# Retention constants and a buffer write issued one stage earlier, and the residual input read inside the out projection

## The chip, the cores and the metric

One NeuronCore of a Trainium2 chip runs the whole program. The metric is the device time in microseconds, as a median over runs. Everything is float32.

## The reference, cut to what matters

The reference is a chain of two transformer-like blocks over 512 tokens of width 1024 (with a context of 256 tokens in the first). The change touches the second half of the first block's mixer and nothing else:

```python
# first block, mixer: two branches over the same normed input, then one projection
r_f, _ = retention_scan(rq, rk, rv, lg_f, states[2], False)       # 4 heads, dk 128, dv 256
r_b, _ = retention_scan(flip(rq), flip(rk), flip(rv), lg_b, states[3], True)
o_ret = head_groupnorm(r_f + flip(r_b)) * silu(heads(rg, 4))
y = sigmoid(m_gla) * (o_gla @ w_branch_gla) + sigmoid(m_ret) * (o_ret @ w_branch_ret)
h_lat = x + g1 * (y @ w_out)
h_lat = h_lat + g2 * hier_moe(...)        # 32 experts, top 2
```

The retention decays depend on positions and heads alone. The kernel keeps them as three constant tables in DRAM: `ret_kdec` (8 KB, one factor per context token, head and direction), `ret_qdec` (512 KB per head once it is spread over the 128 partitions) and `ret_band` (1,792 KB, the banded mask of decays that multiplies the scores). `rope_axial` and `perm_axial` are the tables of the rotary embedding.

## The kernel before, in words

The program is a sequence of stages. Each stage is a `with nc.Block()` in which every engine has its own list of instructions. The end of a block is a barrier of all engines: nothing of the next stage starts, on any engine or on the queue of SyncE (SP), before all have come to it. TensorE writes its products to the eight banks of PSUM in turn (`env.tile()`), VectorE or ScalarE evacuates them. `product_done`, `evacuated` and `bank_ready` are waits on counters of full and free banks.

The large weights come in blocks of 2 MB into a ring of two slots, `wring` (L130, `load_blocks`). Block b may be issued when the last tile that used block b-2 is done; SP waits for that in order, so everything that stands behind it in SP's list waits too. At the end of its list each stage lets `load_blocks` run two blocks ahead of its own. `until` stops it at a given block.

The stages around the change, in order:

1. The GLA branch's `stage_branch`, which ends with VectorE's L831.
2. `stage_ret_project` (from L887): TensorE makes queries (4 tiles), keys (4 tiles), the context's keys by token (2 tiles), eight rotary products of one matmul each (L864), and the values in two halves of 6 tiles each (L951), one weight block for each half: `b_v[0]` and `b_v[1]`. Each of the tiles with weights is a sum over `KD` = 8 products, which the trace shows as 16 float32 matmuls. ScalarE evacuates, VectorE does the rotation (L874 to L881). SP's list: the two rotary tables (L906, L907), then `load_blocks`.
3. `stage_ret_core` (from L955): SP's list begins with a write of 12,288 KB to `y_dram` in DRAM (L983): row 0 of `env.gates` of every partition, repeated. It gives the buffer that the experts will later scatter into finite contents; GpSimd waits for it (`env.y_set`) only in the experts' stage, whose first scatter into it starts at 1192.5 us. Behind it stand `kdec` (L985), `band` (L986), and `qdec` for the four heads (L991), whose third and fourth wait until VectorE has used the first and second. VectorE begins with `v.wait_ge(in_s, 32)`, which is `kdec` and `band` both, then scales the context keys (L1002). TensorE makes the eight state products from these (L1060, 32 matmuls), then for each head the scores (L1067) and the outputs (L1076, L1079). VectorE multiplies the scores with the band (L1013). At the end come the group norm and transposes, which leave the result in `oT`; `oT` is the memory of `env.h`.
4. The retention branch's `stage_branch`: 24 tiles with weights; it reads `oT` and ends with VectorE's L835.
5. `load_tokens` (L2589): a block of its own, in which SP loads `x` (2,048 KB) into `env.h` again (L2596) and waits for it. The other engines have nothing in it.
6. `stage_out`: TensorE's 8 tiles of `y @ w_out` (L1123, 128 matmuls), VectorE's multiplication with the gate (L1112) and the addition to `env.h` (L1114). Its first block of weights has been issued during stage 4, its second at the end of stage 4.
7. The norm before the experts, whose first instruction is ScalarE's at 1085.89 us.

Of the kernel before, what the change touches and what calls it, by code (L numbers as in the profile page):

```python
# [20 lines left out]
ALU = mybir.AluOpType  # L21
# [3 lines left out]
P = 128  # L25
D = 1024
KD = D // P
S = 512
NT = S // P
# [855 lines left out]
def stage_ret_project(env, R):  # L885

    nc, hT, dram = env.nc, env.hT, env.dram  # L887
    q_t = env.tiles(4)
    b_q = env.take_block(q_t[-1])
    k_t = env.tiles(4)  # L890
    kc_t = env.tiles(NCT)
    b_k = env.take_block(kc_t[-1])
    r_t = env.tiles(8)
    v_t, b_v = [], []
    for half in range(2):
        v_t.append(env.tiles(NCH))
        b_v.append(env.take_block(v_t[half][-1]))
    tab_in, cos_s, rope_s = env.sem("ret_tab_in"), env.sem("ret_cos"), env.sem("ret_rope")
    with ExitStack() as st:
        sn = st.enter_context(nc.sbuf_tensor("r_sn", [P, 2, S], F32))  # L900
        tab = st.enter_context(nc.sbuf_tensor("r_tab", [P, 2, S], F32))
        perm = st.enter_context(nc.sbuf_tensor("r_perm", [P, P], F32))
        with nc.Block() as block:
            @block.sync
            def _(sp):
                nc.sync.dma_start(tab[:], dram["rope_axial"]).then_inc(tab_in, 16)  # L906
                nc.sync.dma_start(perm[:], dram["perm_axial"]).then_inc(tab_in, 16)  # L907
                load_blocks(env, sp)

            @block.scalar  # L910
            def _(act):
                for j, t in enumerate(q_t + k_t):
                    product_done(env, act, t)
                    nc.scalar.activation(R.qk[:, j, :], env.ps[:, t[0], :], ACT.Copy).then_inc(env.bank_free[t[0]], 1)
                for i, t in enumerate(kc_t):
                    product_done(env, act, t)
                    nc.scalar.activation(R.kc[:, i, :], env.ps[:, t[0], :], ACT.Copy).then_inc(env.bank_free[t[0]], 1)
                for half in range(2):
                    for i, t in enumerate(v_t[half]):
                        product_done(env, act, t)  # L920
                        nc.scalar.activation(R.v[:, i, half * WBLK:(half + 1) * WBLK], env.ps[:, t[0], :],
                                             ACT.Copy).then_inc(env.bank_free[t[0]], 1)

            @block.vector
            def _(v):
                v.wait_ge(tab_in, 32)
                rope_dve(env, v, r_t, lambda j: R.qk[:, j, :], tab, sn, cos_s, rope_s)

            @block.tensor
            def _(pe):  # L930
                w = block_view(env, pe, b_q)
                for j, t in enumerate(q_t):
                    project(env, pe, t, env.ps[:, t[0], :], w, j * P, (j + 1) * P, lambda k: hT[:, k, 0:S])
                w = block_view(env, pe, b_k)
                for j, t in enumerate(k_t):
                    project(env, pe, t, env.ps[:, t[0], :], w, j * P, (j + 1) * P, lambda k: hT[:, k, 0:S])
                for i, t in enumerate(kc_t):
                    by_token(env, pe, t, WBLK, w, NT + i)
                pe.wait_ge(tab_in, 32)
                rope_mm(env, pe, r_t, perm[:], lambda j: R.qk[:, j, :], lambda j: evacuated(env, pe, (q_t + k_t)[j]))  # L940
                for half in range(2):
                    w = block_view(env, pe, b_v[half])
                    for i, t in enumerate(v_t[half]):
                        by_token(env, pe, t, WBLK, w, i)
# [11 lines left out]
def stage_ret_core(env, R, oT):  # L956
# [3 lines left out]
    st_t = [[env.tile() for d in range(2)] for hd in range(H1)]  # L960
    plan = [([env.tile() for _ in range(NT)], [env.tile() for _ in range(NT)]) for hd in range(H1)]
    fin = env.tiles(2 * H1)
    in_s, kd_s, qd_s, bn_s, mv_s, rms_s, inv_s, nrm_s, o_s = (env.sem("rc_" + n) for n in (
        "in", "kd", "qd", "bn", "mv", "rms", "inv", "nrm", "o"))
    qdec_in = [env.sem(f"rc_qdec_in{i}") for i in range(2)]
    with ExitStack() as stk:
        T = lambda n, s: stk.enter_context(nc.sbuf_tensor("rc_" + n, s, F32))
        band = T("band", [P, H1, 896])
        qdec = T("qdec", [P, 2, 2, S])
        kdec = T("kdec", [P, 2 * H1, NCT])  # L970
        kd = T("kd", [P, 2, 2, NCT, DK])
        st = T("st", [P, H1, 2, DV])
        qd = T("qd", [P, 2, S])
# [6 lines left out]
        with nc.Block() as block:  # L980
            @block.sync
            def _(sp):
                nc.sync.dma_start(env.dram["y_dram"].rearrange("(b p) d -> p b d", p=P),  # L983
                                  env.gates[:, 0, :].unsqueeze(1).broadcast_to([P, NB, D])).then_inc(env.y_set, 16)
                nc.sync.dma_start(kdec[:], dram["ret_kdec"]).then_inc(in_s, 16)  # L985
                nc.sync.dma_start(band[:], dram["ret_band"]).then_inc(in_s, 16)  # L986
                for hd in range(H1):
                    if hd >= 2:
                        sp.wait_ge(qd_s, 2 * (hd - 1))
                    row = dram["ret_qdec"][hd:hd + 1].broadcast_to([P, 2, S])  # L990
                    nc.sync.dma_start(qdec[:, hd % 2], row).then_inc(qdec_in[hd % 2], 16)  # L991
                load_blocks(env, sp)

            @block.vector
            def _(v):
                v.wait_ge(in_s, 32)
                for hd in range(H1):
                    for d in range(2):
                        if hd >= 2:
# [4 lines left out]
                for hd in range(H1):  # L1004
                    sc, ov = plan[hd]
                    if hd >= 1:
                        product_done(env, v, plan[hd - 1][1][-1])
                    v.wait_ge(qdec_in[hd % 2], 16 * (hd // 2 + 1))
                    for d in range(2):
                        nc.vector.tensor_tensor(qd[:, d, :], R.qk[:, hd, :], qdec[:, hd % 2, d, :], ALU.mult).then_inc(qd_s, 1)  # L1010
                    for J, t in enumerate(sc):
                        product_done(env, v, t)
                        nc.vector.tensor_tensor(pm[:, J, :], env.ps[:, t[0], :], band[:, hd, 384 - J * P:384 - J * P + S],  # L1013
                                                ALU.mult).then_inc(env.bank_free[t[0]], 1)
                    for I, t in enumerate(ov):
                        product_done(env, v, t)
                        nc.vector.bn_stats(bn[:, hd * NT + I, :], env.ps[:, t[0], 0:DV]).then_inc(bn_s, 1)
# [66 lines left out]

def stage_out(env, name, src, gate):

    nc = env.nc
    tl = [env.tiles(NT) for _ in range(2)]  # L1090
    bl = [env.take_block(t[-1]) for t in tl]
    g_s = env.sem(name + "_sum")
    with ExitStack() as st:
        tmp = st.enter_context(nc.sbuf_tensor(name + "_tmp", [P, 2 * NT, WBLK], F32))
        with nc.Block() as block:
            @block.sync
            def _(sp):
                load_blocks(env, sp)

            @block.vector  # L1100
            def _(v):
                for half in range(2):
                    cs = slice(half * WBLK, (half + 1) * WBLK)
                    for i, t in enumerate(tl[half]):
                        product_done(env, v, t)
                        got = env.ps[:, t[0], :]
                        if gate is None:
                            nc.vector.tensor_tensor(env.h[:, i, cs], env.h[:, i, cs], got, ALU.add).then_inc(
                                env.bank_free[t[0]], 1)
                        else:  # L1110
                            x = tmp[:, half * NT + i, :]
                            nc.vector.tensor_tensor(x, env.gates[:, gate, cs], got, ALU.mult).then_inc(env.bank_free[t[0]], 1)  # L1112
                            evacuated(env, v, t)
                            nc.vector.tensor_tensor(env.h[:, i, cs], env.h[:, i, cs], x, ALU.add).then_inc(g_s, 1)  # L1114

            @block.tensor
            def _(pe):
# [1468 lines left out]
            env.blocks.append(a[i])  # L2586


def load_tokens(env, name, src):  # L2589

    nc = env.nc
    done = env.sem(name)
    with nc.Block() as block:
        @block.sync
        def _(sp):
            nc.sync.dma_start(env.h[:], src.rearrange("(t p) d -> p t d", p=P)).then_inc(done, 16)  # L2596
            sp.wait_ge(done, 16)


def first_mixer(env):  # L2600
    nc = env.nc
    gain = lambda n: (lambda j: env.gain[:, n, j:j + 1])
# [24 lines left out]
    with ExitStack() as own:  # L2627
        A = lambda n, s: own.enter_context(nc.sbuf_tensor(n, s, F32))
        R = Bufs()
        R.qk, R.kc, R.v = A("ret_qk", [P, 2 * H1, S]), A("ret_kc", [P, NCT, H1 * DK]), A("ret_v", [P, NCH, D])  # L2630
        stage_ret_project(env, R)
        stage_ret_core(env, R, oT)
    stage_branch(env, "ret", oT, yT, False)
    load_tokens(env, "x_again", env.dram["x"])
    env.hold = True
    stage_out(env, "mix_out", yT, 0)
    branch.close()
    mod.close()

# [248 lines left out]
```

## Time and profile before

| | us |
|---|---|
| median of 3 runs | 3281.82 |
| lowest and highest | 3277.95 and 3285.40 |
| the profiled execution's own time | 3285.16 |
| its span | 3283.3 |
| TensorE busy | 2788.1 (85% of the span) |
| VectorE busy | 1478.0 (45%) |
| ScalarE busy | 490.4 (15%) |
| GpSimd busy | 734.7 (22%) |
| mean granted TensorE clock | 0.929 |

The page of the profile cuts the span into 40 equal slices of 82 us and gives each engine's busy share in tenths. Further views are asked of the same execution: the timeline (instructions of each engine in order of time, merged where one follows another without a pause), windows (busy time of each engine in given stretches, with the clock that TensorE was granted and the DMA engines' share), and the DMA issues with the time from issue to landing. All times are microseconds from the start of the span. 1.00 of the granted clock is 2.4 GHz, 0.50 is 1.2 GHz.

### The profile page before, as it was taken

Reading aid. Unit: us, or ns where it says so; the run is one execution under the profiler, and the core shown is the slowest. Engines: PE = TensorE matmul, PEld = TensorE weight load, DVE = VectorE, ACT = ScalarE, POOL = GpSimd, SP = SyncE. Lnnn points to the kernel's source line nnn. Section 1 sums busy time; section 2 is a strip of 40 time slices with the busy share of each in tenths; the row PEclk is TensorE's granted clock in tenths of the full one; section 3 lists DMA queues with packets and bytes.
Section 4 is the critical chain, followed back from the end, with each engine's and each line's share of the span. In section 5 each row is a group of like instructions: output and inputs, shape, how many; then the busy total and the mean of one; then the engine's idle time right before and its main releaser. Section 6 shows DMA issues by size and latency. Waiting matters only on the chain. (4 is left out here: it accounts for less than half of the span.)

```text
span 3283.3 us, 30222 instructions
## 1 busy us (share of the span) xinstructions
PE 2788.1 (85%) x10080; PEld 1561.4 (48%) x10080; DVE 1478.0 (45%) x3007; ACT 490.4 (15%) x1015; POOL 734.7 (22%) x652
## 2 busy tenths in 40 slices
PE   7997899976998689977979989998990578888877
PEld 3446434435443433323435568887880443333333
DVE  1126200102201322212137429888668987777762
ACT  2124100000100111113026321111110210000002
POOL 0000000000000012220000002655457036666650
PEclk9897998997999689988989999998995999999998
DMA  5100251123022479971210026999999249999992
GB/s 201 48 30 24 103 204 59 51 98 155 26 77 77 171 320 409 391 300 72 77 65 7 1 84 243 416 402 346 419 416 372 81 193 413 413 414 413 413 363 86
DMA packets 133341, 693.93 MB, mean 211 GB/s; under 512 B 19571, under 2 KB 20979, under 8 KB 105587
## 3 DMA queue, kind: packets, MB, share of 16 engines
q1 hardware_dynamic: 50644, 408.32, 31.4%
q0 software_dynamic: 81792, 281.07, 21.7%
q10 hardware_dynamic: 800, 3.15, 0.3%
q8 instruction: 65, 1.06, 0.1%
q14 instruction: 40, 0.33, 0.0%
HBM read 701.90 MB, written 48.23 MB: 228 GB/s over the span
## 5 line engine op out<-in xcount | busy, mean ns | idle before, releaser
L428 PE MATMUL ps<-hT,wring 128*128 128x256 f32 (+1 forms) x2576 | 763.3, 458 | 30.3 <-ACT pk_g L2249 14.4
L428 PEld LDWEIGHTS ps<-hT,wring 128*128 128x128 f32 x2576 | 491.1, 191 | 297.3 <-issue 253.5
L2468 PE MATMUL ps<-pm_v_rows,pm_weighted 128*128 128x512 f32 x1024 | 464.7, 603 | 62.0 <-DVE pm_weighted L2518 44.3
L2143 POOL DMA_INDIRECT pk_ring<-in_peer_u,pk_rows x256 | 311.3, 1216 | 760.6 <-DVEq L2357 537.0
L2285 DVE CUSTOM_DVE_ANT_0 pk_ring<-pk_ring,mem_x 128x1024 f32<-128x1024 f32 x256 | 309.7, 1224 | 104.5 <-DMA pk_ring<-in_peer_u,pk_rows 99.6
L2468 PEld LDWEIGHTS ps<-pm_v_rows,pm_weighted 128*128 128x128 f32 x1024 | 185.7, 189 | 340.4 <-issue 227.6
L2436 POOL DMA_INDIRECT hT<-in_peer_v,pm_idxs x192 | 251.7, 1311 | 211.5 <-PE ps L2456 107.8
L1416 POOL COPY ex_idx<-row_token 128x1 uint32 (+1 forms) x24 | 4.5, 186 | 1283.4 <-PEq L1548 1149.9
L2524 DVE SCALAR_TENSOR_TENSOR h_tok<-hT,gates,h_tok 128x1024 f32<-128x1024 f32 x192 | 244.6, 1282 | 100.3 <-DMA hT<-in_peer_v,pm_idxs 65.0
L951 PE MATMUL ps<-wring,hT 128*128 128x512 f32 (+1 forms) x544 | 213.9, 555 | 1.2 <-PEq L376 1.2
L1603 DVE TENSOR_SCALAR hT<-ps,gain,ada 128x128 f32<-128x128 f32 x192 | 63.4, 405 | 216.2 <-PE ps L1504 216.2
L428 PE MATMUL ps<-hT,pk_u 128*128 128x256 f32 x704 | 153.8, 379 | 0.0
L951 PEld LDWEIGHTS ps<-wring,hT 128*128 128x128 f32 x544 | 98.4, 190 | 116.2 <-issue 116.2
L428 PEld LDWEIGHTS ps<-hT,pk_u 128*128 128x128 f32 x704 | 133.7, 190 | 18.3
L1514 PE MATMUL ps<-ex_gu,hT 128*64 128x512 f32 x512 | 115.8, 606 | 5.5 <-DVE hT L1603 4.3
L428 PE MATMUL ps<-h_tok,wring 128*128 128x512 f32 x256 | 112.1, 599 | 0.0
L2249 ACT ACTIVATE pk_g<-ps 128x256 f32<-128x256 f32 x128 | 48.3, 385 | 395.6 <-PE ps L428 307.8
L2456 PE MATMUL ps<-hT 128*128 128x128 f32 x512 | 65.4, 281 | 41.6 <-ACT pm_coef_table L2486 21.3
L1533 PE MATMUL ps<-ex_dn,ex_hidT 128*64 128x512 f32 x384 | 87.7, 598 | 1.2 <-issue 1.2
L548 PE MATMUL ps<-wring,hT 128*128 128x512 f32 x192 | 85.6, 609 | 0.0
L346 ACT ACTIVATE ple_xn<-h_tok 128x1024 f32<-128x1024 f32 x4 | 4.2, 1042 | 528.3 <-PEq L2404 528.3
L2449 PE MATMUL ps<-pm_coef_table 128*128 128x512 f32 x8 | 5.9, 897 | 90.6 <-DVE pm_coef_table L2492 90.6
(422 smaller groups left out, 3014.0 us busy)
## 6 DMA issues: line engine op xcount, KB each, us to landing
ex_gu<-in_experts SPq DMA_DIRECT2D x32, 2048.0 KB
pm_v_rows<-in_peer_v SPq DMA_DIRECT2D x64, 1024.0 KB
ex_dn<-in_experts SPq DMA_DIRECT2D x48, 1024.0 KB
wring<-in_w_in SPq DMA_DIRECT2D x21, 2048.0 KB, 7.8
wring<-in_peer_uT SPq DMA_DIRECT2D x21, 2048.0 KB
wring<-in_experts SPq DMA_DIRECT2D x16, 2048.0 KB
ada_w<-in_w_ada SPq DMA_DIRECT2D x12, 2048.0 KB
pk_u<-in_peer_uT SPq DMA_DIRECT2D x11, 2048.0 KB
```

The source lines that it names most:

```text
L428: mm = env.nc.tensor.matmul(out, w[:, k, lo:hi], rhs(k), start=(k == 0), stop=(k == KD - 1))
L548: mm = nc.tensor.matmul(env.ps[:, t[0], :], hT[:, k, i * P:(i + 1) * P], w[:, k, :], start=(k == 0), stop=(k == KD - 1))
L951: mm = env.nc.tensor.matmul(env.ps[:, t[0], 0:n], env.hT[:, k, i * P:(i + 1) * P], w[:, k, lo:lo + n], start=(k == 0), stop=(k == KD - 1))
L1514: mm = nc.tensor.matmul(env.ps[r, GU[s], :], xT[:, s, k, r], wg[n % GUS][h][:, k, :], start=(k == 0), stop=(k == KD - 1))
L1533: mm = nc.tensor.matmul(env.ps[r, DOWN[q], :], hidT[:, s, k, r], wd[s][h][:, k, q * WBLK:(q + 1) * WBLK], start=(k == 0), stop=(k == EFT - 1))
L1603: nc.vector.tensor_scalar(xT[:, s, k, :], env.ps[:, ROWS[n], j * P:(j + 1) * P], gain(k), shift(k), ALU.mult, ALU.add).then_inc(xT_done, 1)
L2143: nc.gpsimd.indirect_dma_start(ring[:, n % RING, :], None, dram["peer_u"], bass.IndirectOffsetOnAxis(ap=rows[:, n // SLOTS, n % SLOTS:n % ...
L2285: V.tensor_tensor_reduce(ring[:, r, :], ring[:, r, :], xg[:, t, :], 1.0, 0.0, ALU.mult, ALU.add, G.coef[:, t, n % SLOTS:n % SLOTS + 1]).th ...
L2436: nc.gpsimd.indirect_dma_start(ring[r], None, dram["peer_v"], bass.IndirectOffsetOnAxis(ap=idx[:, half, r:r + 1], axis=0)).then_inc(got[r] ...
L2456: mm = nc.tensor.matmul(env.ps[:, CB[2 * q + j // 4], j % 4 * PK:(j % 4 + 1) * PK], A[q][:, j, :], B[q][:, j, :], start=True, stop=True)
L2468: mm = nc.tensor.matmul(env.ps[:, OUT[n], :], W[q][:, j * DS + t * P:j * DS + (t + 1) * P], vr[j // 2][:, j % 2 * D + half * WBLK:j % 2 * ...
L2524: nc.vector.scalar_tensor_tensor(env.h[:, t, :], ring[r], coef[:, t, bass.ds(RING * i + n // GT, 1)], env.h[:, t, :], ALU.mult, ALU.add).t ...
```

## The change

`band`, `qdec` and `kdec` become members of `R`, allocated for both retention stages, with semaphores of their own. SP's list of `stage_ret_project` gets the constants behind the load of the first half's value weights, and the write of `y_dram` behind the load of the second half's. `stage_ret_core` keeps only `qdec` of the third and fourth head; VectorE's first wait is for `kdec` alone, and it waits for the band ahead of the first multiplication with it. `load_tokens` is removed with its block: `stage_out` issues the load of `x` first in SP's list, and VectorE waits for it ahead of each addition.

```diff
@@ stage_ret_project, SP's list
                 nc.sync.dma_start(tab[:], dram["rope_axial"]).then_inc(tab_in, 16)
                 nc.sync.dma_start(perm[:], dram["perm_axial"]).then_inc(tab_in, 16)
+                load_blocks(env, sp, until=b_v[0] + 1)
+                nc.sync.dma_start(R.kdec[:], dram["ret_kdec"]).then_inc(R.kdec_in, 16)
+                for hd in range(2):
+                    row = dram["ret_qdec"][hd:hd + 1].broadcast_to([P, 2, S])
+                    nc.sync.dma_start(R.qdec[:, hd], row).then_inc(R.qdec_in[hd], 16)
+                nc.sync.dma_start(R.band[:], dram["ret_band"]).then_inc(R.band_in, 16)
+                load_blocks(env, sp, until=b_v[1] + 1)
+                nc.sync.dma_start(dram["y_dram"].rearrange("(b p) d -> p b d", p=P),
+                                  env.gates[:, 0, :].unsqueeze(1).broadcast_to([P, NB, D])).then_inc(env.y_set, 16)
                 load_blocks(env, sp)
@@ stage_ret_core
-                nc.sync.dma_start(env.dram["y_dram"].rearrange("(b p) d -> p b d", p=P),
-                                  env.gates[:, 0, :].unsqueeze(1).broadcast_to([P, NB, D])).then_inc(env.y_set, 16)
-                nc.sync.dma_start(kdec[:], dram["ret_kdec"]).then_inc(in_s, 16)
-                nc.sync.dma_start(band[:], dram["ret_band"]).then_inc(in_s, 16)
-                for hd in range(H1):
-                    if hd >= 2:
-                        sp.wait_ge(qd_s, 2 * (hd - 1))
+                for hd in range(2, H1):
+                    sp.wait_ge(qd_s, 2 * (hd - 1))
                     row = dram["ret_qdec"][hd:hd + 1].broadcast_to([P, 2, S])
                     nc.sync.dma_start(qdec[:, hd % 2], row).then_inc(qdec_in[hd % 2], 16)
                 load_blocks(env, sp)
 
             @block.vector
             def _(v):
-                v.wait_ge(in_s, 32)
+                v.wait_ge(R.kdec_in, 16)
...
+                    if hd == 0:
+                        v.wait_ge(R.band_in, 16)
                     for J, t in enumerate(sc):
@@ stage_out
             def _(sp):
+                nc.sync.dma_start(env.h[:], again.rearrange("(t p) d -> p t d", p=P)).then_inc(again_in, 16)
                 load_blocks(env, sp)
...
-                        if gate is None:
...
+                        x = tmp[:, half * NT + i, :]
+                        nc.vector.tensor_tensor(x, env.gates[:, gate, cs], got, ALU.mult).then_inc(env.bank_free[t[0]], 1)
+                        evacuated(env, v, t)
+                        v.wait_ge(again_in, 16)
+                        nc.vector.tensor_tensor(env.h[:, i, cs], env.h[:, i, cs], x, ALU.add).then_inc(g_s, 1)
@@ first_mixer
-    load_tokens(env, "x_again", env.dram["x"])
     env.hold = True
-    stage_out(env, "mix_out", yT, 0)
+    stage_out(env, "mix_out", yT, 0, env.dram["x"])
```

## Rows read from the trace of the kernel before

**Rows 1.** The 40 slices of the page: TensorE busy tenths, granted clock.

```profile
PE   7997899976998689977979989998990578888877
...
PEclk9897998997999689988989999998995999999998
```

**Rows 2.** Windows: length, busy time by engine, clock, DMA share, GB/s.

```profile
710.00:720.00 10.00, 10.00 (x24) 4.37 (x23) 0.00 (x0) 0.60 (x1) 0.00 (x0) 1.00 0.00 0
...
730.00:740.00 10.00, 0.00 (x0) 0.00 (x0) 0.00 (x0) 0.00 (x0) 0.00 (x0) 0.50 1.02 421
...
760.00:770.00 10.00, 4.23 (x10) 3.43 (x11) 2.56 (x12) 0.77 (x2) 0.00 (x0) 0.50 0.65 270
770.00:780.00 10.00, 10.00 (x35) 7.10 (x35) 4.86 (x11) 2.31 (x6) 0.00 (x0) 0.90 0.15 54
...
1020.00:1030.00 10.00, 3.41 (x4) 1.51 (x5) 0.00 (x0) 0.00 (x0) 0.00 (x0) 0.50 0.49 202
1030.00:1040.00 10.00, 10.00 (x23) 4.47 (x22) 1.38 (x2) 0.00 (x0) 0.00 (x0) 0.93 0.00 0
```

**Rows 3.** Timeline, 715 to 780 us: start, duration, instruction, idle before.

```profile
721.97 0.60 ACT L921 ACTIVATE ret_v<-ps 128x512 f32<-128x512 f32 x1 [6.27 <-PE ps L951]
722.82 0.41 SPq L983 DMA_DIRECT2D y_dram_out<-gates  x1
723.27 23.89 SPq L985 DMA_DIRECT2D rc_kdec<-in_ret_kdec  x1
...
765.23 1.66 DVE L1002 TENSOR_SCALAR rc_kd<-ret_kc,rc_kdec 128x128 f32<-128x128 f32 x8 [115.51 <-DMA rc_band<-in_ret_band]
...
765.77 10.22 PE L1060 MATMUL ps<-ret_v,rc_kd 128*128 128x256 f32 x32 [43.84 <-DVE rc_kd L1002]
...
775.83 3.60 PE L1067 MATMUL ps<-ret_qk 128*128 128x512 f32 x8
```

**Rows 4.** DMA issues, 715 to 770 us: size each, time to landing.

```profile
y_dram_out<-gates SPq DMA_DIRECT2D x1, 12288.0 KB, 38.1
wring<-in_w_in SPq DMA_DIRECT2D x1, 2048.0 KB, 9.1
rc_band<-in_ret_band SPq DMA_DIRECT2D x1, 1792.0 KB, 18.0
...
rc_kdec<-in_ret_kdec SPq DMA_DIRECT2D x1, 8.0 KB, 37.8
```

**Rows 5.** Timeline, 1008 to 1090 us.

```profile
1013.71 0.69 DVE L835 TENSOR_TENSOR yT<-yT,ret_merge 128x512 f32<-128x512 f32 x1
1014.67 0.38 SPq L2596 DMA_DIRECT2D h_tok<-in_x  x1
...
1026.59 5.62 PE L1123 MATMUL ps<-wring,yT 128*128 128x512 f32 x7 [13.64 <-PEq L2593]
...
1077.54 6.60 PE L1123 MATMUL ps<-wring,yT 128*128 128x512 f32 x15
```

**Rows 6.** DMA issues of the whole span: the second load of x.

```profile
h_tok<-in_x SPq DMA_DIRECT2D x1, 2048.0 KB, 11.3
```

**Rows 7.** Timeline, 562 to 620 us: barrier ahead of retention projection.

```profile
562.60 0.69 DVE L831 TENSOR_TENSOR yT<-gla_merge,ps 128x512 f32<-128x512 f32 x1 [6.18 <-PE ps L428]
...
563.76 55.17 PE L428 MATMUL ps<-hT,wring 128*128 128x512 f32 x128 [1.20 <-PEq L797]
```

**Rows 8.** Timeline of SyncE's queue, two stretches: the value weights' loads.

```profile
591.49 0.33 SPq L130 DMA_DIRECT2D wring<-in_w_in  x1
...
632.69 89.59 SPq L130 DMA_DIRECT2D wring<-in_w_in  x3
```

**Rows 9.** Timeline of TensorE at 2690 us: burst behind a pause.

```profile
2690.62 7.13 PE L2468 MATMUL ps<-pm_v_rows,pm_weighted 128*128 128x512 f32 x16 [1.91 <-DMA pm_v_rows<-in_peer_v]
```

**Rows 10.** Window of 50 us: TensorE beside busy DMA engines.

```profile
2050.00:2100.00 50.00, 50.00 (x234) 44.01 (x232) 42.96 (x120) 5.76 (x15) 31.60 (x23) 1.00 1.02 418
```

**Rows 11.** DMA issues of the whole span: stores by SyncE.

```profile
g_dram_out<-pk_g SPq DMA_DIRECT2D x32, 512.0 KB
```

More of the change, by code:

```diff
@@ L962, in stage_ret_core @@
     fin = env.tiles(2 * H1)
-    in_s, kd_s, qd_s, bn_s, mv_s, rms_s, inv_s, nrm_s, o_s = (env.sem("rc_" + n) for n in (
-        "in", "kd", "qd", "bn", "mv", "rms", "inv", "nrm", "o"))
-    qdec_in = [env.sem(f"rc_qdec_in{i}") for i in range(2)]
+    kd_s, qd_s, bn_s, mv_s, rms_s, inv_s, nrm_s, o_s = (env.sem("rc_" + n) for n in (
+        "kd", "qd", "bn", "mv", "rms", "inv", "nrm", "o"))
+    band, qdec, kdec, qdec_in = R.band, R.qdec, R.kdec, R.qdec_in
     with ExitStack() as stk:
         T = lambda n, s: stk.enter_context(nc.sbuf_tensor("rc_" + n, s, F32))
-        band = T("band", [P, H1, 896])
-        qdec = T("qdec", [P, 2, 2, S])
-        kdec = T("kdec", [P, 2 * H1, NCT])
         kd = T("kd", [P, 2, 2, NCT, DK])
@@ L1083, in _, with stage_out @@
                             lambda ch, j: pe.wait_ge(nrm_s, (j // 2) * NT + ch + 1))
-def stage_out(env, name, src, gate):
+def stage_out(env, name, src, gate, again):
     nc = env.nc
@@ L1091, in stage_out @@
     bl = [env.take_block(t[-1]) for t in tl]
-    g_s = env.sem(name + "_sum")
+    g_s, again_in = env.sem(name + "_sum"), env.sem(name + "_again")
     with ExitStack() as st:
@@ L1106, in _ @@
                         got = env.ps[:, t[0], :]
-                        if gate is None:
[L1108 to L1114, printed above, removed]
+                        x = tmp[:, half * NT + i, :]
[3 more added lines that the diff above has]
+                        nc.vector.tensor_tensor(env.h[:, i, cs], env.h[:, i, cs], x, ALU.add).then_inc(g_s, 1)
             @block.tensor
@@ L2586, in stream @@
             env.blocks.append(a[i])
[L2589 to L2597, printed above, removed]
 def first_mixer(env):
@@ L2630, in first_mixer @@
         R.qk, R.kc, R.v = A("ret_qk", [P, 2 * H1, S]), A("ret_kc", [P, NCT, H1 * DK]), A("ret_v", [P, NCH, D])
+        R.band, R.qdec, R.kdec = A("rc_band", [P, H1, 896]), A("rc_qdec", [P, 2, 2, S]), A("rc_kdec", [P, 2 * H1, NCT])
+        R.qdec_in = [env.sem(f"rc_qdec_in{i}") for i in range(2)]
+        R.kdec_in, R.band_in = env.sem("rc_kdec_in"), env.sem("rc_band_in")
         stage_ret_project(env, R)
```

## The prediction

> **What bounds the kernel now.** I read the 40 slices first [rows 1]. TensorE is busy in seven or more tenths of nearly every slice, so a gain has to come from a stretch where it stands still. The ninth slice (657 to 739 us) holds 7 tenths, the tenth 6 at a clock of 0.7, the thirteenth 8 (985 to 1067); these five hold the stages that the change touches. Then the windows of 10 us [rows 2]: from 730 on no engine computes anything while the DMA engines are full (421 GB/s, share 1.02), TensorE comes back only between 760 and 770, and at clock 0.50, which is 1.2 GHz. A second, smaller hole lies at 1020 to 1030, with the clock at 0.50 again.
>
> The timeline says what ends each hole. In the first, VectorE's first scaling of the keys waits for the band to land, TensorE waits for that scaling, and its pause is 43.84 us [rows 3]. The DMA view gives the cause of the cause [rows 4]: the constants of 8 KB took 37.8 us to land, since they stand in one queue behind the write of 12,288 KB that took 38.1; the band landed at 747.21 + 18.0 = 765.2, and there VectorE starts. In the second hole TensorE pauses 13.64 us [rows 5], and the load of x issued at 1014.67 takes 11.3 us [rows 6], to 1025.97. Its block lets nobody pass before that.
>
> **Part 1: the constants and the write go to the projection.** Nothing is taken away: kdec, band, two qdec and the write are issued by SP in both versions, and only their place changes.
>
> What goes from the path. VectorE starts on the keys at 765.23. Afterwards its start is set by the barrier alone: ScalarE's last evacuation ends at 722.57, SP issues its first instruction at 722.82 [rows 3]. I take 722.9 for VectorE (0.25 to 0.9 us behind the barrier's last instruction; 0.47 is what TensorE needed at another barrier, 563.29 to 563.76 [rows 7]). Gain 765.23 - 722.9 = 42.3 us, bounds 41.7 to 42.4. TensorE follows 0.54 us behind VectorE, now as then, so its pause shrinks from 43.84 to about 1.5 us. What is late next is TensorE itself: VectorE makes 8 scalings in 1.66 us, two feed one state product.
>
> The clock. The eight state products are 32 matmuls of 256 columns and take from 765.77 to the first score at 775.83, 10.06 us [rows 3], partly at 1.2 GHz [rows 2]. At 2.4 GHz a matmul of 256 columns costs 50 / 234 = 0.214 us [rows 10], so 32 are 6.8 us. If the pause of 1.5 us leaves the clock at 2.4 GHz, 3.2 us go too; bounds 0 and 3.2. I take 3.2, by the nearest row: behind a pause of 1.91 us 16 matmuls of 512 columns took 7.13 us, 0.446 each [rows 9], and the full pace is 55.17 / 128 = 0.431 [rows 7].
>
> What the move costs in the projection. SP's order there is: load of value half 1 at 591.49, then the constants at once, load of half 2 at 632.69, then the write, then the next load [rows 8]. Constants: 8 + 2 x 512 + 1,792 KB = 2.8 MB behind a load of 2 MB. The 12,288 KB took 38.1 us behind such a load [rows 4], so 4.8 MB need some 15 us, and they land by about 607, at the latest by 591.8 + 38 = 630: 93 us before the core begins. SP is free again well before 632.69. The load of half 2 stands ahead of the write, as the load at 721.96 stood ahead of it before and still took only 9.1 us [rows 4]. It lands at 642. TensorE needs it when the first half of the values is done: the rotary products begin at 632.5, just ahead of the issue at 632.69 [rows 8]; they take 8 x 2 x 0.43 = 6.9 us, then 6 tiles x 16 x 0.43 = 41.3 us, so 680.7. Even if the load landed only with the write, at 633.1 + 38.1 = 671, it would be in time. SP is to issue the next load at 680.7 as well, and the write has landed 9 us earlier; that load is for the branch behind the whole core. Nothing of this is on the path: 0.
>
> The write beside busy engines. It ran alone before [rows 2], so its effect on TensorE isn't in its own rows. From one side it can give nothing back (0). From the other: with DMA share 1.02 and stores of 512 KB among the transfers [rows 11], TensorE issued 234 matmuls in 50 us, 0.2137 us each [rows 10], half of 0.431 within 1%. One per cent of 38 us is 0.4 us. I take 0.
>
> In the core: qdec of heads 0 and 1 has landed; of heads 2 and 3 it is issued when VectorE has used the first two, as before, without the write ahead of it, and is needed two heads later. The band's wait passes at once. The new waits of VectorE hold nothing up. Cost 0. SP has only the third and fourth qdec and the next loads behind its wait.
>
> **Part 2: x is read inside the out projection.** TensorE starts when the barrier lets it: VectorE's L835 ends at 1014.40 and 0.47 us later is 1014.87 [rows 5, 7]. It started at 1026.59. Gain 11.7 us, bounds 11.3 (0.9 us for the barrier) and 11.9. Its first weights are there, issued in the branch; the second block is needed only 4 tiles x 6.9 = 27.5 us later.
>
> The added wait: SP issues the load at the same point of the stage, 1014.67, and it lands at 1025.97 on the old time scale. VectorE has its first product at 1014.87 + 6.87 + 0.2 = 1021.9, multiplies (0.69 us) and waits at the addition until 1026.0. Behind that wait stands its multiplication of tile 2, whose product comes at 1028.8. So VectorE is free 2 us before it is needed, and TensorE has 8 banks for 8 tiles, so it waits for nobody. Should the load take 11 us longer, VectorE still catches up at 1.4 us of work for each tile of 6.9 us. Cost 0.
>
> The clock again. The 128 matmuls take from 1026.59 to 1084.14, 57.55 us [rows 5]; at the full pace 55.17 [rows 7] they would take 2.4 less. The pause shrinks from 13.64 us to 1.9, which is the pause of [rows 9]. I take 2.4; bounds 0 and 2.4.
>
> The Trainium skill, page "TensorE: Matmul & The Clock Gate", section "HAM oscillation — how this bites in real kernels", warns that pauses between bursts send the array's clock back to half rate, so that every burst begins cold. If both shortened pauses did that, the sum would lose its two terms for the clock. The row at 2690 speaks against it.
>
> **Sum.** 42.3 + 3.2 + 11.7 + 2.4 = 59.6 us. Behind the out projection every stage begins at a barrier, and no transfer of a later stage is issued ahead of it, so the rest shifts as a whole. Against the profiled execution: 3285.16 - 59.6 = 3225.6. That execution lies 3.3 us above the median of the three runs, near the highest; the median is the better base for a median: 3281.82 - 59.6 = 3222.2, taken as 3222.
>
> **Rivals.**
>
> A. The clock falls in both short pauses. Then TensorE's stretches begin at 1.2 GHz as now [rows 2], the gain is 54.0 and the time 3227.8. For it: both pauses are longer than 1.20 us, behind which the clock held [rows 7]. Against it: 1.91 us [rows 9]. Chance 0.10.
>
> B. The write is no longer free. It runs beside TensorE, ScalarE and VectorE and beside what the engines fetch for themselves. If it held TensorE for as long as it lasts, 38 us come back: 3222 + 38 = 3260; a third of it gives 3235. For it: its own row shows no working engine beside it. Against: the pace of 0.2137 at share 1.02 [rows 10]. The Trainium skill, page "SBUF — State Buffer", section "Who interferes with whom", says that a DMA never contends with a compute engine; by it the price is 0, and the trace agrees for TensorE to 1%. Chance 0.05.
>
> C. The hole is not set by the queue alone: VectorE's start or a qdec turns out late for a reason that the band's wait hides today. The bound is one landing such as the band's, 18.0 us [rows 4]; gain 41.6, time 3240.2. Against: the constants have 93 us of slack. Chance 0.04.
>
> D. Slower than before. The pause of 43.8 us is a rest for TensorE. Without it the engine runs from 564 to 1084 us with short pauses only. If the chip answered with 1.2 GHz, every microsecond of full-rate work costs one more. It decides from 59.6 + 6.6 = 66 us of such work at half rate; over core and branch, some 240 us, the time would be 3222 + 240 = 3462. Against: slices 32 to 39 hold a clock of 0.9 or more and the window at 2050 one of 1.00 through busy stretches [rows 1, 10]. Chance 0.02.
>
> E. The change doesn't move the wait: some part of the core still waits on the write, through the order of the queue. The gain would be that of part 2 alone, 14.1 us: 3267.7. The diff leaves nothing but two qdec in that list. Chance 0.02.
>
> **How the numbers follow.** Forecast 0.77, A 0.10, B 0.05, C 0.04, D 0.02, E 0.02. The forecast's own range: bounds of the barrier terms -1 and +0.3 us, and the runs' spread of 3.9 below and 3.6 above the median, some more for where the clock rises in the later stages: 3213 to 3230. With A whole and the nearer third of B the range becomes 3212 to 3235; what it leaves out is most of B and C, D and E, and a tail of the forecast, together below 0.2. A measurement of this kernel can tell 0.2%, 6.6 us, from no change. Faster by more than that: all but D and a remnant, 0.96; within: 0.01; slower: 0.03.
>
> **What would show it.** Right: TensorE's pause ahead of the state products 1 to 2 us; no idle window with a full DMA share; the first score some 45.5 us earlier, near 730.3; the write issued near 633 beside a TensorE at clock 1.00 and its landing in about 38 us; the pause ahead of the out projection near 1.9 us; ScalarE's first instruction of the experts' norm near 1026.3 instead of 1085.89; the first addition to h waiting for a DMA some 3 us, once. Wrong: state products over 8 us, or an out projection over 56 us (A); tiles of values over 6.9 us each, or the rotary stretch longer, between 633 and 671 (B); VectorE waiting for qdec (C); clock 0.50 inside the branch (D).

## The result, and the profile after

The changed kernel takes 3221.98 us (median of 4 runs, 3220.94 to 3230.48) against 3279.89 us for the kernel before (4 runs, 3273.98 to 3285.40): ratio 0.9831, 95% interval 0.9818 to 0.9844. The predicted time was 3222. In a second comparison on another occasion the same kernel had 3220.43 us (5 runs) against 3278.62 (9 runs), ratio 0.9812, interval 0.9797 to 0.9827. By the medians the gain is 57.9 us in the one and 58.2 in the other; 59.6 had been worked out. The ratios are estimated from the single runs and differ by up to 0.1% from the quotient of the medians (0.9823 and 0.9822); by them the gain is 55 and 62 us, each to about 5 us. The profiled execution after took 3222.66 us, its span is 3220.8, which is 62.5 less than before.

The slices of the page after, TensorE's busy tenths and its granted clock; a slice is now 80.5 us:

```profile
PE   6997899999997599959889989998980678888877
...
PEclk8997998999999699979999999999995999999998
```

The tenth and eleventh slice (725 to 886 us) hold 9 and 9, where before the ninth and tenth held 7 and 6 [rows 1].

The timeline after, around the start of the retention core (start, duration, instruction, idle before it). It answers to [rows 3]:

```profile
723.12 0.60 ACT L930 ACTIVATE ret_v<-ps 128x512 f32<-128x512 f32 x1 [6.27 <-PE ps L960]
724.03 2.19 DVE L1003 TENSOR_SCALAR rc_kd<-ret_kc,rc_kdec 128x128 f32<-128x128 f32 x10 [73.15 <-PEq L903]
...
724.56 7.17 PE L1063 MATMUL ps<-ret_v,rc_kd 128*128 128x256 f32 x32 [1.48 <-DVE rc_kd L1003]
...
731.57 3.60 PE L1070 MATMUL ps<-ret_qk 128*128 128x512 f32 x8
```

VectorE starts 0.31 us behind ScalarE's last evacuation (723.12 + 0.60 to 724.03), released by the barrier and by no DMA. TensorE's pause is 1.48 us instead of 43.84. The state products take 731.57 - 724.56 = 7.01 us instead of 10.06.

SyncE's queue in the projection, its moved instructions among them (answers to [rows 8]), and below it the DMA issues from 592 to 634 us and of the write (answers to [rows 4]):

```profile
592.65 0.33 SPq L130 DMA_DIRECT2D wring<-in_w_in  x1
593.02 0.43 SPq L909 DMA_DIRECT2D rc_kdec<-in_ret_kdec  x1
593.50 0.96 SPq L912 DMA_DIRECT2D rc_qdec<-in_ret_qdec  x2
594.49 0.49 SPq L913 DMA_DIRECT2D rc_band<-in_ret_band  x1
633.85 0.33 SPq L130 DMA_DIRECT2D wring<-in_w_in  x1
634.22 0.44 SPq L915 DMA_DIRECT2D y_dram_out<-gates  x1
681.92 0.33 SPq L130 DMA_DIRECT2D wring<-in_w_in  x1
```

```profile
wring<-in_w_in SPq DMA_DIRECT2D x2, 2048.0 KB, 9.7
rc_band<-in_ret_band SPq DMA_DIRECT2D x1, 1792.0 KB, 13.7
...
rc_kdec<-in_ret_kdec SPq DMA_DIRECT2D x1, 8.0 KB, 7.9
```

```profile
y_dram_out<-gates SPq DMA_DIRECT2D x1, 12288.0 KB, 39.2
```

The constants have landed by 594.49 + 13.7 = 608.2, 116 us before they are wanted. The write has landed at 634.22 + 39.2 = 673.4, 8.5 us before SyncE issues the next load.

The windows after, of the stretch in which the write runs beside the projection, and of the start of the core (length, busy time and instructions by engine, clock, DMA share, GB/s). They answer to [rows 2]:

```profile
650.00:660.00 10.00, 10.00 (x25) 4.50 (x24) 0.77 (x2) 0.60 (x1) 0.00 (x0) 1.00 1.02 422
660.00:670.00 10.00, 10.00 (x24) 4.40 (x24) 0.00 (x0) 1.19 (x2) 0.00 (x0) 1.00 1.02 420
720.00:730.00 10.00, 8.52 (x33) 5.88 (x32) 4.78 (x18) 2.53 (x6) 0.00 (x0) 1.00 0.58 208
730.00:740.00 10.00, 10.00 (x41) 7.29 (x40) 3.21 (x6) 1.53 (x4) 0.00 (x0) 1.00 0.18 56
```

The full DMA share of 1.02 that stood beside idle engines before now stands beside a TensorE that is busy for 10.00 of 10 us at clock 1.00. From the issue at 633.85 to that at 681.92 the rotary products and the first half of the values take 48.07 us; 8 x 2 + 6 x 16 matmuls at 0.43 us are 48.2. From one load of value weights to the end of the projection it is 89.27 us in both kernels (632.69 to 721.96 before, 633.85 to 723.12 after).

The out projection after, answering to [rows 5] and [rows 6]:

```profile
968.20 0.69 DVE L835 TENSOR_TENSOR yT<-yT,ret_merge 128x512 f32<-128x512 f32 x1
969.16 0.38 SPq L1101 DMA_DIRECT2D h_tok<-in_x  x1
...
969.37 20.84 PE L1124 MATMUL ps<-wring,yT 128*128 128x512 f32 x48 [1.92 <-PEq L797]
...
976.51 0.69 DVE L1112 TENSOR_TENSOR mix_out_tmp<-gates,ps 128x512 f32<-128x512 f32 x1 [7.61 <-PE ps L1124]
...
980.57 0.69 DVE L1115 TENSOR_TENSOR h_tok<-h_tok,mix_out_tmp 128x512 f32<-128x512 f32 x1 [3.37 <-DMA h_tok<-in_x]
...
983.37 0.69 DVE L1112 TENSOR_TENSOR mix_out_tmp<-gates,ps 128x512 f32<-128x512 f32 x1 [2.12 <-PE ps L1124]
```

```profile
h_tok<-in_x SPq DMA_DIRECT2D x1, 2048.0 KB, 11.3
```

TensorE starts 0.48 us behind VectorE's last instruction, after a pause of 1.92 us instead of 13.64. VectorE waits 3.37 us for x, once, and is ready 2.1 us before the second product. The 128 matmuls end at 1024.54, after 55.17 us instead of 57.55. ScalarE begins the experts' norm at 1026.29; it was 1085.89, so 59.60 us are gained up to there.

### The profile page after: what moved, and what is told of

The parts are those of the page before. It is cut to its first block and busy times, and to the rows that moved or that the text cites. A ratio compares the mean times of both kernels' runs of the same rounds, so it can differ in the third digit from the quotient of the medians.

```text
span 3220.8 us, 30219 instructions
## 1 busy us (share of the span) xinstructions
PE 2779.2 (86%) x10080; PEld 1558.2 (48%) x10080; DVE 1478.4 (46%) x3007; ACT 489.8 (15%) x1015; POOL 732.9 (23%) x652
## 5 line engine op out<-in xcount | busy, mean ns | idle before, releaser
L2144 POOL DMA_INDIRECT pk_ring<-in_peer_u,pk_rows x256 | 304.0, 1187 | 765.3 <-DVEq L2358 538.9
L2437 POOL DMA_INDIRECT hT<-in_peer_v,pm_idxs x192 | 258.4, 1346 | 206.3 <-PE ps L2457 107.8
L2457 PEld LDWEIGHTS ps<-hT 128*128 128x128 f32 x512 | 59.6, 191 | 48.5 <-ACT pm_coef_table L2487 47.9
```

What stands on the lines that cost most here:

```text
L2144: nc.gpsimd.indirect_dma_start(ring[:, n % RING, :], None, dram["peer_u"], bass.IndirectOffsetOnAxis(ap=rows[:, n // SLOTS, n % SLOTS:n % ...
L2437: nc.gpsimd.indirect_dma_start(ring[r], None, dram["peer_v"], bass.IndirectOffsetOnAxis(ap=idx[:, half, r:r + 1], axis=0)).then_inc(got[r] ...
L2457: mm = nc.tensor.matmul(env.ps[:, CB[2 * q + j // 4], j % 4 * PK:(j % 4 + 1) * PK], A[q][:, j, :], B[q][:, j, :], start=True, stop=True)
```

## Experiments

All times are medians; the ratios are against the kernel before, run on the same chip in the same round. There were three rounds, on three chips: experiments 1 to 3 (the kernel before at 3278.01 us), experiment 4 with the first kernels of 5 and 6 (3278.62), and the other kernels of 5 and 6 (3275.39). Medians of different rounds are best compared by their ratios.

**1. Each part alone.** The first kernel has only the change of `stage_out`, the second only that of the two retention stages:

```diff
# the first kernel: the kernel before, with
+                nc.sync.dma_start(env.h[:], again.rearrange("(t p) d -> p t d", p=P)).then_inc(again_in, 16)
                 load_blocks(env, sp)
-    load_tokens(env, "x_again", env.dram["x"])
# the second kernel: the changed kernel, with
+    load_tokens(env, "x_again", env.dram["x"])
-                nc.sync.dma_start(env.h[:], again.rearrange("(t p) d -> p t d", p=P)).then_inc(again_in, 16)
```

> Part 2 alone: the load of x moves into the out projection, the constants and the write stay where they were before. Theory (two separate pauses, each worth its own barrier term and clock term): TensorE's pause ahead of the out projection 1.9 us instead of 13.64, the 128 matmuls 55.2 us instead of 57.55, the pause of 43.8 us ahead of the state products unchanged; 14.1 us faster than before, ratio 0.9957. Rival (the gain of the whole change is one thing, such as a clock that stays up over all stages, and doesn't split): less than 7 us, ratio over 0.998. Rival (VectorE's wait for x holds TensorE): the out projection over 58 us.

> Part 1 alone: the constants and the write move into the projection, x is loaded in a block of its own as before. Theory: pause ahead of the state products 1.5 us, state products 7.0 us, and from there as before; 45.5 us faster, ratio 0.9861; with part 2 alone it adds up to the whole change (59.6 us). Rival (part 2 gains more once part 1 is there, or the other way): the two parts differ from the whole by over 5 us.

Measured: 3265.2 us, 0.9956 (0.9941 to 0.9971), and 3233.55 us, 0.9864 (0.9844 to 0.9884). That is 12.8 and 44.5 us, 57.3 together, beside 57.9 and 58.2 for the whole. Within the intervals of some 5 to 7 us the two parts add up and neither needs the other. The timeline of the kernel with part 2 alone still has the old hole in the core:

```profile
765.31 1.66 DVE L1002 TENSOR_SCALAR rc_kd<-ret_kc,rc_kdec 128x128 f32<-128x128 f32 x8 [115.24 <-DMA rc_band<-in_ret_band]
...
765.85 8.74 PE L1060 MATMUL ps<-ret_v,rc_kd 128*128 128x256 f32 x32 [43.56 <-DVE rc_kd L1002]
...
774.43 3.60 PE L1067 MATMUL ps<-ret_qk 128*128 128x512 f32 x8
```

But the state products behind it take 774.43 - 765.85 = 8.58 us here, not 10.06. In the kernel with part 1 alone they take 7.01, and its out projection, still behind a pause of 13.76 us, 56.97 us.

**2. Only the order of the queue.** The kernel before, with the write moved to the end of the core's list:

```diff
-                nc.sync.dma_start(env.dram["y_dram"]...)       # first in stage_ret_core
                 nc.sync.dma_start(kdec[:], dram["ret_kdec"]).then_inc(in_s, 16)
...
                 load_blocks(env, sp)
+                nc.sync.dma_start(env.dram["y_dram"]...)
```

> The kernel before with one change: the write of 12,288 KB stands last in SyncE's list of the retention core instead of first; all constants stay in the core. Theory (the hole is the constants' place in the queue behind the write): band and kdec land behind the 2,048 KB load issued at 722 alone, near 736; VectorE starts there, some 29 us earlier; the pause of TensorE about 15 us, so its clock falls to 0.50 and the state products still take 10 us; 29 us faster, ratio 0.991. Of the whole part 1 (45.5) that leaves 13.5 us for the place of the constants and 3 us for the clock. Rival (the hole is the constants' own transfer, or the barrier): pause above 35 us, under 9 us gained.

Measured: 3245.98 us, 0.9904 (0.9886 to 0.9921), 32.0 us faster than before. The DMA issues of this kernel from 715 to 800 us:

```profile
y_dram_out<-gates SPq DMA_DIRECT2D x1, 12288.0 KB, 34.7
wring<-in_w_in SPq DMA_DIRECT2D x1, 2048.0 KB, 7.8
...
rc_band<-in_ret_band SPq DMA_DIRECT2D x1, 1792.0 KB, 10.9
rc_kdec<-in_ret_kdec SPq DMA_DIRECT2D x1, 8.0 KB, 7.1
```

kdec lands in 7.1 us where it took 37.8 [rows 4], the band at 723.51 + 10.9 = 734.4, VectorE starts at 734.49. TensorE's pause is 12.78 us and its state products take 8.60, where 10 had been expected. So of the 43.8 us, 31.1 were the write's place in the queue, and only 11.3 more (12.78 to 1.48) needed the move to another stage. The write's place has two effects here: what stands behind it lands late, and SyncE can't even issue the band until 747.21, since the issue of kdec held it for 23.89 us [rows 3]; without the write ahead the band is issued at 723.51. No run tried the constants in the queue of another engine.

**3. The clock without the wait.** The kernel before, in which TensorE computes something else while it waits for the band:

```diff
             def _(pe):
+                bank_ready(env, pe, st_t[0][0])
+                for n in range(49):
+                    nc.tensor.matmul(env.ps[:, st_t[0][0][0], :], R.qk[:, 0, 0:P], R.qk[:, 0, :], start=True, stop=True)
                 for hd in range(H1):
```

> The kernel before, with 49 additional matmuls of 512 columns (98 as the trace counts them, some 42 us) on TensorE ahead of its first state product; their results are overwritten, all waits stay. Theory (the clock term of 3.2 us is the pause's effect on TensorE's clock): the wait for the band still ends at 765, but the window 730 to 760 shows clock 1.00 and the 32 matmuls of the state products take 7.0 us instead of 10.06; 3 us faster, ratio 0.999, which the times hardly tell but the trace does. Rival (the state products are fed slowly by VectorE or evacuated slowly by ScalarE): still 10 us at clock 1.00. Rival (TensorE needs the rest of the pause): clock below 1.00 between 770 and 1010 and the stage of the branch longer than 168 us.

Measured: 3277.21 us, 0.9997 (0.9987 to 1.0008): no difference that can be told, as expected; the interval holds the 3 us that were expected, and none. The windows show why the trace is needed:

```profile
740.00:750.00 10.00, 10.00 (x24) 4.37 (x23) 0.00 (x0) 0.00 (x0) 0.00 (x0) 1.00 1.02 422
...
760.00:770.00 10.00, 8.29 (x24) 4.17 (x23) 2.14 (x10) 0.38 (x1) 0.00 (x0) 1.00 0.82 333
770.00:780.00 10.00, 10.00 (x41) 7.29 (x40) 5.41 (x12) 2.70 (x7) 0.00 (x0) 1.00 0.15 54
```

```profile
767.69 2.19 DVE L1002 TENSOR_SCALAR rc_kd<-ret_kc,rc_kdec 128x128 f32<-128x128 f32 x10 [116.64 <-DMA rc_band<-in_ret_band]
...
768.22 7.17 PE L1063 MATMUL ps<-ret_v,rc_kd 128*128 128x256 f32 x32 [1.72 <-DVE rc_kd L1002]
...
775.23 3.60 PE L1070 MATMUL ps<-ret_qk 128*128 128x512 f32 x8
```

The wait is the same, VectorE still starts when the band has landed (here at 767.69), but the clock stays at 1.00 and the state products take 775.23 - 768.22 = 7.01 us, as in the changed kernel. VectorE and ScalarE feed and evacuate them in both cases alike, so the difference to 10.06 (or 8.58) is the clock. Nor did TensorE need the rest: it ran from 565 to 831 us without a pause over 1.72 us, and the branch behind it took its 167 us (844.64 to 1011.37, 166.7).

**4. The changed kernel again, and the constants behind the write.**

```diff
                 load_blocks(env, sp, until=b_v[1] + 1)
                 nc.sync.dma_start(dram["y_dram"]...)
+                nc.sync.dma_start(R.kdec[:], dram["ret_kdec"]).then_inc(R.kdec_in, 16)     # and qdec, band: moved here
```

> The changed kernel again, for comparison with the others on this chip: 3222 us, ratio 0.983 against before; pause ahead of the state products 1.5 us, ahead of the out projection 1.9 us.

> The changed kernel with the constants behind the write in the projection's list instead of ahead of it: the same order in the queue as in the kernel before, but a stage earlier. Theory (what counts is the landing before the core begins, not the order): the constants land near 682, 41 us before VectorE needs kdec; no pause, time as the changed kernel within 0.2%, ratio 0.983. Rival (whatever stands behind the write waits for longer than the write): VectorE waits for kdec or band in the core, over 5 us lost.

Measured: 3220.43 us, 0.9812 (0.9797 to 0.9827), and 3222.84 us, 0.9826 (0.9809 to 0.9842): the same. kdec again takes 39.1 us behind the write, from an issue at 632.29, and the band 19.3 from 659.48, so both have landed by 679, and VectorE wants them at 721.6. The order that cost 31 us in the core costs nothing a stage earlier.

**5. The write ahead of a load that TensorE needs.** Three kernels, the changed kernel with the write ahead of the load of the second half's value weights; in the second SyncE first waits for the keys, as the load does; in the third the write is made twice, one after the other:

```diff
+                product_done(env, sp, env.block_tile[b_v[1] - 2])     # second and third kernel
+                nc.sync.dma_start(dram["y_dram"]...)                  # all three
+                sp.wait_ge(env.y_set, 16)                             # third kernel
+                nc.sync.dma_start(dram["y_dram"]...)                  # third kernel
                 load_blocks(env, sp, until=b_v[1] + 1)
```

> The changed kernel with the write ahead of the load of the second half's value weights, which TensorE needs 48 us after the write is issued. Theory: the load lands with or just behind the write, 39.2 us + 2 MB at some 420 GB/s = 5 us + 2 us, about 680 to 682, where TensorE needs it at 681.9: 0 to 2 us lost, so the slack of 9 us that the prediction gave to a load landing with the write is nearly used up, but the time stays within 0.2% of the changed kernel. Rival (the load is kept back until SyncE's descriptors for the write are through and then takes its 9 us): a pause of TensorE of 2 us or more between the two halves, visible as a pause ahead of the second half's first matmul.

> The run before this (write ahead of the values' load in the list) issued the write at 594.75 already, since SyncE's wait for the keys stands in the load. Here SyncE waits for the keys first, then issues the write, then the load of the second half's value weights, all near 633. Theory: the two transfers together take what they took in the other order, 39 us from the first issue, so the load lands near 673 and TensorE needs it at 682: no pause, time as the changed kernel. That is the 9 us of slack that the prediction gave. Rival (a load behind the write is delayed by more than the write's own bytes): a pause ahead of the second half's first matmul.

> As the run before, but the write is made twice, the second when the first has landed, and both stand ahead of the load of the value weights: 24,576 KB beside the projection. Theory (queued bytes in front of a load that TensorE needs are what costs, and beside busy engines a transfer costs nothing): first write landed near 634 + 35, second near 704, the load some 5 us later, near 709; TensorE pauses 27 us ahead of the second half's values (needed at 682), its matmuls keep 0.43 us each up to there; 27 to 30 us slower than the changed kernel, ratio against before 0.991. Rival (contention of the write with busy engines): each tile of six values' tiles longer than 6.87 us while the writes run, from 634 to 682.

Measured: 3220.01 us, 0.9824 (0.9810 to 0.9837); 3215.24, 0.9821 (0.9806 to 0.9836); 3241.62, 0.9896 (0.9881 to 0.9911). The first didn't test what it was for: without a wait of its own the write was issued at 594.75 and landed at 638.2 (43.4 us, with 4.8 MB ahead of it), only 4.6 us after the load was issued at 633.53, so the load took 9.5 us. It shows a place even further from any need. The expectation for it was also wrong in its sum: it added the load's 5 us to 39.2, which had a load ahead of it already. In the second the load stands behind the write, is issued at 631.77 and takes 39.5 us, until 671.3. TensorE needs it at 679.5 and doesn't pause. In the third, timeline of SyncE, DMA issue of the load, and windows:

```profile
632.81 0.41 SPq L915 DMA_DIRECT2D y_dram_out<-gates  x1
665.25 0.39 SPq L918 DMA_DIRECT2D y_dram_out<-gates  x1
665.68 81.61 SPq L130 DMA_DIRECT2D wring<-in_w_in  x3
```

```profile
wring<-in_w_in SPq DMA_DIRECT2D x1, 2048.0 KB, 37.9
```

```profile
650.00:660.00 10.00, 10.00 (x24) 4.37 (x23) 0.00 (x0) 0.60 (x1) 0.00 (x0) 1.00 1.02 409
670.00:680.00 10.00, 10.00 (x25) 4.50 (x24) 0.00 (x0) 0.60 (x1) 0.00 (x0) 1.00 1.02 410
...
690.00:700.00 10.00, 0.00 (x0) 0.00 (x0) 0.00 (x0) 0.00 (x0) 0.00 (x0) 0.50 1.03 378
```

The load lands at 665.68 + 37.9 = 703.6 and TensorE starts its second half at 703.65, after a pause of 22.8 us; 27 had been expected, since the write takes 33 us where no load is ahead of it. By the ratios the kernel is 21 to 28 us slower than the changed one (0.9896 against 0.9831 and 0.9812, of 3280); by the medians it is 26 us slower than the second kernel, which ran in its round (3241.62 against 3215.24). While the 24 MB are written and TensorE has its weights, it remains busy 10.00 of 10 us at clock 1.00; that ends at 680.85, when the weights are missing. From the keys' end to that of the first half of the values it is 680.85 - 632.81 = 48.04 us, as without. So what costs is the place of the bytes in the queue; their flow beside busy engines costs nothing that the trace can show.

**6. The same idea at two more places.** In the first kernel the latent expansion's weights and tables (2.5 MB) are issued in the stage ahead of it; in the second, in addition, the router's eight constants in the norm ahead of the router. Both stages of the changed kernel began with TensorE waiting for them (4.7 and 6.5 us):

```diff
# stage_second_project, SP's list
+                load_blocks(env, sp, until=blks[3] + 1)
+                nc.sync.dma_start(M.le_wq[:], dram["w_uq"]).then_inc(M.le_in, 16)          # and wkv, tab, perm
                 load_blocks(env, sp)
# stage_norm, SP's list
+                for to, what, sem in also:                                                # the router's eight
+                    nc.sync.dma_start(to, what).then_inc(sem, 16)
                 load_blocks(env, sp)
```

> The changed kernel and the same idea once more: the weights, tables and permutation of the second block's latent expansion (2.5 MB) are issued in the stage ahead of it, behind the load of its fourth weight block. Theory: TensorE's pause there falls from 4.7 us (5.7 in the kernel before) to the 1 to 2 us of VectorE's last evacuation; 3 to 5 us faster than the changed kernel, 3218, ratio against before 0.982. Rival (the evacuations and VectorE's norm end last there): under 1 us.

> The version with the expansion's weights issued a stage earlier, and in the same way the router's eight constants, issued in the norm ahead of it. Theory: TensorE's pause ahead of the router's first product falls from 6.5 us to 1 or 2, since the last of eight issues of 0.43 us each and its landing end there now; 4 to 5 us faster than the version before it, 9 to 11 faster than the changed kernel: 3210, ratio against before 0.979. Rival (the loads delay the store of the normed rows, or the experts' first gather ends last): no gain behind the router.

Measured: 3216.04 us, 0.9807 (0.9794 to 0.9821), which the times can't tell from the changed kernel's 0.9812; and 3203.84 us, 0.9777 (0.9764 to 0.9791), which they can: the interval lies below both of the changed kernel's. By the ratios the step from the first kernel to the second is 10 us (0.0030 of 3277), where 4 to 5 were expected. The router's start in it:

```profile
1045.23 1.28 ACT L1273 ACT_TABLE_LOAD   x1 [0.27 <-PEq L376]
...
1045.41 1.95 PE L1249 MATMUL ps<-rt_w,hT 128*128 128x36 f32 x16 [1.27 <-PEq L376]
...
1049.97 3.63 PE L1249 MATMUL ps<-rt_w,hT 128*128 128x36 f32 x16
...
1058.42 0.31 DVE L1286 COPY rt_lg<-ps 128x144 f32<-128x144 f32 x1 [13.04 <-PE ps L1250]
```

TensorE's pause there is 1.27 us instead of 6.5. Its first 16 products of 36 columns take 1.95 us and the next 16 take 1.98, where each 16 took 3.63 in the changed kernel, whose granted clock is 0.50 from 1045 to 1060 us. From 1049.97 on they take 3.63 here too, at a clock of 0.50, although TensorE has had no pause since 1045.41: the clock fell while TensorE was working on these products. From the end of the norm's transposes to the last product it is 1058.29 - 1044.14 = 14.2 us instead of 1063.74 - 1040.65 = 23.1: 8.9 us gained, of which the pause is 5.2 and most of the rest the clock. The expectation had counted the pause alone. In the expansion the stage's start to TensorE's first product with weights shrinks from 14.49 to 10.54 us.

## Why the prediction was right

- **The barrier instead of the landing** (42.3 us): right. The pause fell by 42.36 us, and VectorE started 0.31 us behind the barrier's last instruction (0.33 had been taken). Experiment 2 splits it: 31.1 for the queue's order, 11.3 for the stage.
- **The clock in the state products** (3.2 us, bounds 0 and 3.2): right in kind, shown by experiment 3. Its size belongs to an execution, not to the kernel. The executions with a long pause ahead of them took 10.06, 8.58 and 8.60 us, and all without one 7.01. The profile before had the dearest; the term is 1.6 to 3.05. That is the term most clearly mis-sized for a median, and it has the size of what is missing from 59.6 us (57.9 and 58.2 measured). That it is the cause of that difference isn't shown: the intervals of the two comparisons are wider than it.
- **The constants and the write in the projection** (0): right. The constants landed at 608.2 where 607 was worked out, 116 us ahead of their use (93 was the bound for the latest landing); the write landed at 673.4 instead of 671, and the projection kept its 89.27 us. Rival B (contention, up to 38 us) falls, and experiment 5 puts twice the bytes beside the same work without a trace of it.
- **Order against landing**: the statement that even a load behind the write would be in time is shown by the second kernel of experiment 5 (671.3 against 679.5), and the third shows the point from which it isn't.
- **x inside the out projection** (11.7 us, and 2.4 for the clock): right, 11.71 and 2.38. In other executions with the pause still there the out projection took 56.96 to 57.15 us, so the clock is worth 1.8 to 2.4. VectorE's wait was 3.37 us and hid as worked out.
- **The rest shifts as a whole**: right to 2.9 us. Up to the experts' norm 59.60 us were gained, over the span 62.5. The 59.60 match the forecast partly by luck: the four terms gave 59.5, the after execution had already lost 1.2 us ahead of the change (the projection starts at 564.91 instead of 563.76), and it won about as much in the branch, which took 166.5 us instead of 167.6. The sum had put both at nothing. Behind the norm some 2.4 us more were won at the pause ahead of the second block's memory tables (90.6 to 88.25 us), which the change doesn't touch. In other executions of the same and of nearly the same kernels this pause was 84 to 90 us long, which is one reason why single spans differ by more than the smaller terms do.
- **The hit to 0.02 us** (3222 against 3221.98): luck. The gain by the medians was 1.7 us smaller than forecast, and the kernel before came out 1.9 us lower (3279.89) than the median of three that the forecast started from (3281.82), since a fourth run of 3273.98 joined. The single runs of the changed kernel lie 9.5 us apart. What the runs confirm is the sum to a few microseconds, and its parts in the traces.
- **Rivals A, C, D, E**: A falls with the state products at 7.01 us and the out projection at 55.17; C with a VectorE released by the barrier; D with experiment 3 and with a branch that took no longer than before; E with the pause of 1.48 us. The sign given for D, a clock of 0.50 inside the branch, would have misled: in both kernels the branch begins at a lower clock (0.50 from 845 to 850 us before, 0.72 from 801 to 806 after, then 1.00). It stands behind the pauses of 4.12 us ahead of the core's last transposes and of 3.88 (after: 3.22) ahead of the branch, which the change doesn't touch.

The Trainium skill's warning on pauses (page "TensorE: Matmul & The Clock Gate", section "HAM oscillation — how this bites in real kernels") agrees with the long pauses of this kernel (43.56 us: 8.58 us of state products). Behind those of 1.48 and 1.92 us the clock stayed at 1.00; the page's own example has longer waits than these, so the two don't contradict each other.

## What to carry to other kernels

A small transfer can be as late as a large one ahead of it in its queue: 8 KB took 37.8 us behind 12,288 KB, and 7.1 with the write behind it. Look in the trace at what the first instruction of a stage waits for, and issue it in the stage before, behind that stage's own loads; there the order hardly matters, and the large transfer runs free beside busy engines as long as no load that TensorE needs soon stands behind it. A long pause that goes also gives back what TensorE lost at 1.2 GHz behind it, 1.6 to 3 us here; in the router, with its many short products, some 3.7 us came beside the 5.2 of the pause.

## What the runs showed of the hardware

The write of 12,288 KB took 32.4 to 34.7 us with no load ahead of it and 38.1 to 39.4 behind a load of 2 MB; windows that it fills alone show 406 to 424 GB/s. Whatever SyncE issued directly behind the write held it for long: kdec 23.89 us before [rows 3] and 24.29 with the constants behind the write in the projection (experiment 4), a load of 2 MB 19.69 and 19.15 us in the second and third kernel of experiment 5. In the changed kernel the next issue behind the write comes only at 681.92, when it has landed, and none of the issues took more than 0.5 us. After a long pause the time for which TensorE stayed slow (its granted clock at 0.50, 1.2 GHz) differed between executions of the same instructions: 10.06 and 8.58 us for the state products behind pauses of 43.84 and 43.56 us.
